# RWKV-7 scan: the decay's running sum over a chunk made by TensorE with a triangular matrix instead of by VectorE's scan, with a new order of the work around it

## What is computed

```python
w_lo = jnp.tanh(jnp.einsum("bld,zdr->zblr", xw, P["rw_w1"][j]))
w_raw = (P["rw_w0"][j][:, None, None, :] + jnp.einsum("zblr,zre->zble", w_lo, P["rw_w2"][j])).astype(f32)
decay = jnp.exp(-jnp.exp(-jax.nn.softplus(-w_raw) - 0.5))
...
def step(S, inp):
    r_t, w_t, k_t, v_t, a_t, b_t = inp
    sa = jnp.einsum("bhvk,bhk->bhv", S, a_t)
    S = S * w_t[:, :, None, :] + sa[..., :, None] * b_t[..., None, :] + v_t[..., :, None] * k_t[..., None, :]
    return S, jnp.einsum("bhvk,bhk->bhv", S, r_t)
```

## Time and profile before

| | |
|---|---|
| time, three runs | 3157.86, 3162.32, 3163.5 us; median 3162.32 us |
| profiled execution | 3172.32 us, span 3170.4 us |
| PE / PEld / DVE / ACT / POOL busy | 2754.4 / 1697.8 / 1449.8 / 729.9 / 246.5 us |
| stage of the scan | about 2030 to 2994 us of the span |
| mean granted TensorE clock | 0.932 of full |

### The profile page before, as it was taken

One profiled execution on the slowest core, in us unless ns is written; L12 is line 12 of the kernel. 1 busy time (PEld: TensorE's weight loads), 2 busy tenths in 40 slices (PEclk: granted clock), 3 DMA queues, 4 the chain that ended last, 5 costly groups with the idle time before them and its releaser, 6 DMA issues. The chain is left out here.

```text
span 3170.4 us, 73804 instructions
## 1 busy us (share of the span) xinstructions
PE 2754.4 (87%) x33234; PEld 1697.8 (54%) x33234; DVE 1449.8 (46%) x2139; ACT 729.9 (23%) x1264; POOL 246.5 (8%) x393
## 2 busy tenths in 40 slices
PE   7589999998999968939999999678888888898697
PEld 1155555554344434415555555367777777777543
DVE  0222222223999880051000000289898998988101
ACT  0122122221211110020000001244444545443100
POOL 0000000000000000000000000001121111111100
PEclk9789999998999989969999999789899999999698
DMA  6322222224223105113232323101111111110131
GB/s 239 132 78 83 88 88 84 88 86 133 67 67 100 58 13 194 45 47 102 79 104 86 99 94 97 52 28 32 34 42 38 34 45 35 41 34 27 66 142 60
DMA packets 208118, 242.59 MB, mean 77 GB/s; under 512 B 22439, under 2 KB 158135, under 8 KB 205544
## 3 DMA queue, kind: packets, MB, share of 16 engines
q1 hardware_dynamic: 197100, 196.56, 19.9%
q0 software_dynamic: 10752, 41.95, 3.6%
HBM read 184.97 MB, written 53.49 MB: 75 GB/s over the span
## 5 line engine op out<-in xcount | busy, mean ns | idle before, releaser
L104 PE MATMUL ps<-mix,rw 128*128 128x512 f32 (+1 forms) x2048 | 564.1, 439 | 21.7 <-DMA rw<-in_rw_w_v 5.7
L104 PE MATMUL ps<-hT,hw 128*128 128x512 f32 (+1 forms) x2048 | 561.3, 435 | 6.3 <-DMA hw<-in_hy_w_in 6.3
L104 PEld LDWEIGHTS ps<-mix,rw 128*128 128x128 f32 x2048 | 313.9, 194 | 271.9 <-issue 271.9
L104 PEld LDWEIGHTS ps<-hT,hw 128*128 128x128 f32 x2048 | 312.5, 191 | 252.4 <-issue 252.4
L104 PE MATMUL ps<-ow,oy 128*128 128x512 f32 x640 | 282.5, 604 | 27.5 <-DMA oy<-scratch_y_d 19.6
L1376 POOL TENSOR_SCALAR e_Sd<-e_S,e_pcd 128x64 f32<-128x64 f32 x256 | 163.7, 656 | 787.0 <-DVE e_S L107 319.2
L104 PEld LDWEIGHTS ps<-ow,oy 128*128 128x128 f32 x640 | 123.7, 194 | 185.2 <-issue 162.5
L118 ACT ACT_TABLE_LOAD x90 | 115.5, 1283 | 381.9 <-PE ps L104 276.1
L107 DVE SCALAR_TENSOR_TENSOR mix<-xx,col,hT 128x640 f32<-128x640 f32 x48 | 38.6, 879 | 287.5 <-PE ps L104 287.5
L112 DVE TENSOR_SCALAR hcv<-hpad,hpc 128x641 f32<-128x641 f32 x48 | 29.6, 616 | 305.7 <-ACT hpad L118 305.7
L115 DVE TENSOR_TENSOR rout<-ps,rsig 128x640 f32<-128x640 f32 x16 | 13.2, 824 | 275.2 <-ACT rsig L118 275.2
(11 more groups left out here) (205 smaller groups left out, 4168.8 us busy)
## 6 DMA issues: line engine op xcount, KB each, us to landing
hw<-in_hy_w_in SPq DMA_DIRECT2D x64, 512.0 KB, 4.1
aw<-in_ada_w SPq DMA_DIRECT2D x16, 1536.0 KB, 8.0
scratch_rkvz_d<-rout POOLq DMA_DIRECT2D x64, 320.0 KB, 3.4
scratch_vx_d<-hot POOLq DMA_DIRECT2D x32, 320.0 KB, 3.1
ow<-in_hy_w_out SPq DMA_DIRECT2D x32, 256.0 KB, 2.7
rw<-in_rw_w_r SPq DMA_DIRECT2D x16, 512.0 KB, 3.9
rw<-in_rw_w_k SPq DMA_DIRECT2D x16, 512.0 KB, 4.0
rw<-in_rw_w_v SPq DMA_DIRECT2D x16, 512.0 KB, 4.0
```

What stands on the lines that cost most here:

```text
L104: return nc.tensor.matmul(out, lhsT, rhs, start=first, stop=last)
```

## The change

The decay's raw rate is now made with tokens in the partitions: `rate(j, part)` takes a block of 128 tokens of `wlo` as weights and streams the 128 channels of `e_w2`, and adds the bias with a second product (a matrix with one row of ones per half, `first_rows`, and the row `e_w0`, which is loaded by two small transfers per unit). Both directions use their own half of the rows. `rate*` is one sigmoid of ACT over both directions (two, with the fifth block). `cum(j, d)` then multiplies each block of `e_sg` (as weights, tokens in the partitions) with a triangular matrix of ones within chunks, which gives the running sum with channels in the partitions again, in `wide`. `exps` takes it from there: it writes `e3` by reading the sum of the neighbouring token and puts 1 at the chunk's edge. `scan` is gone from DVE. `e_kr` for d = 0 moves from DVE to ACT (`kr0`). The load of `v` for the next unit waits for one more piece, and the first `e_w0` load waits for a memset of POOL.

```diff
-    ORDER = [("center*", 1), ("sums", 1), ("sb", 1, 0), ("sums*", 1), ("lora", 1, 0, 0), ("W*", 1, 0), ("sb*", 1, 1), ("U", 1, 0), ("std", 1),
...
+    ORDER = [("Z*", 1, 5), ("Q", 1), ("center*", 0), ("sums", 0), ("sb", 0, 1), ("W*", 0, 0), ("sb", 0, 0), ("sums*", 0), ("U", 0, 0), ("Sd", 0, 0),
...
+                    for d in range(2):
+                        sp.dma_start(w0[64 * d:64 * d + 1, :], A["rw_w0"][0, d:d + 1, ch(j)]).then_inc(s_l["w0"], 16)
...
+                def rate(j, part):
+
+                    wide_free("rate", j, part)
+                    pe.wait_ge(s_l["w2"], 16 * (j + 1))
+                    pe.wait_ge(s_l["w0"], 32 * (j + 1))
+                    for b in range(4) if part == 0 else (4,):
+                        for second in range(2):
+                            for d, hh in enumerate(HEADS):
+                                out = ps[:, WIDE + d, b % 4 * P:(b % 4 + 1) * P]
+                                if second:
+                                    last = mm(out, first_rows[hh, :], w0[hh, :], False, True)
+                                else:
+                                    mm(out, G["wlo"][hh, b * P:(b + 1) * P], lw2[hh, :], True, False)
+                    pe_.did(last, ("rate", j, part))
+
+                def sums_over_chunk(j, d):
+                    wide_free("cum", j, d)
+                    for part in range(2):
+                        wait(ac_, "took", "rate", j, part)
+                    for b in range(NT):
+                        last = mm(wide[:, b * P:(b + 1) * P], sg[:, d, b * P:(b + 1) * P], upto[d])
+                    pe_.did(last, ("cum", j, d))
...
+                def rate(j, part):
+                    wait(pe_, "rate", j, part)
+                    if j:
+                        for d in range(2):
+                            wait(dv_, "b", j - 1, d)
+                    at, n = (0, LS) if part == 0 else (LS, LP)
+                    ac_.did(act(sg[:, :, at:at + n], ps[:, WIDE:WIDE + 2, 0:n], ACT.Sigmoid), ("took", "rate", j, part))
...
+                    ac_.did(act(by_chunk(e3)[:, :, own], by_chunk(wide[:, 0:T])[:, :, prior], ACT.Exp, scale=-DECAY_MAX))
+                    ac_.did(act(by_chunk(e3)[:, :, edge], one.to_broadcast([P, NC]), ACT.Copy))
+                    ac_.did(act(e2[d][:, :], wide[:, 0:T], ACT.Exp, scale=DECAY_MAX), ("e2", j, d))
+                    ac_.did(act(e1, wide[:, 0:T], ACT.Exp, scale=-DECAY_MAX), ("exp", j, d))
+                    ac_.note(("took", "cum", j, d))
...
-                def scan(j, d):
-                    e1, e3 = ab[j % 3][:, 1, d, :], ab[j % 3][:, 0, d, :]
-                    for h in range(2):
-                        wait(ac_, "took", "lora", j, 0, h)
-                    if j >= 3:
-                        wait(pe_, "O", j - 3)
-                    dv_.did(vec.tensor_tensor_scan(e1, chunk, sg[d][:, :], 0.0, MUL, ADD), ("cum", j, d))
-                    wait(dv_, "cum", j, d)
-                    if d == 0:
-                        dv_.did(tt(e3, e1, sg[d][:, :], SUB), ("c", j, d))
-                    else:
-                        tot = chunks(e1)[:, :, C - 1:C].to_broadcast([P, NC, C])
-                        dv_.did(tt(chunks(e3), tot, chunks(e1), SUB), ("left", j))
-                        wait(dv_, "left", j)
-                        dv_.did(tt(e1, e3, sg[d][:, :], ADD), ("c", j, d))
```

More of the change, by code:

```diff
@@ L1161, in rwkv_scan @@
     T_ = lambda n: tab[:, TAB[n][0]:TAB[n][1]]
-    ident, heads, center, heads2, eye2, chunk = (T_(n) for n in ("ident", "heads", "center", "heads2", "eye2", "chunk"))
+    ident, heads, center, heads2, eye2, one, first_rows = (T_(n) for n in ("ident", "heads", "center", "heads2", "eye2", "one", "first_rows"))
+    upto = [T_("upto_f"), T_("upto_b")]
     between = T_("between").rearrange("p (l n) -> p l n", l=LEVELS)
@@ L1229, in rwkv_scan @@
                 jobs.append(piece)
-            if piece[0] in ("center", "lora", "sums", "spread", "bonus"):
+            if piece[0] in ("center", "rate", "cum", "lora", "sums", "spread", "bonus"):
                 wide_before[piece] = wide_last
@@ L1262, in rwkv_scan @@
         TAKER = {"sb": dv_, "sk": dv_, "V": ac_, "tb": ac_, "tk": ac_, "CT": ac_, "T": dv_, "Y": dv_, "Z": dv_, "O": ac_,
-                 "center": ac_, "lora": ac_, "sums": dv_, "spread": dv_, "bonus": dv_}
+                 "center": ac_, "rate": ac_, "cum": ac_, "lora": ac_, "sums": dv_, "spread": dv_, "bonus": dv_}
         def waiter(eng):
@@ L1313, in after_values @@
                         wait(pe_, "V", i)
+                        wait(dv_, "took", "bonus", i)
                         load_row("v", i + 1)
@@ L1317, in after_lora @@
                     if (q, h) == (1, 1) and j + 1 < KE:
-                        wait(pe_, "lora", j, 0, 1)
+                        wait(pe_, "rate", j, 0)
+                        wait(pe_, "rate", j, 1)
                         wait(pe_, "lora", j, 1, 1)
@@ L1580, in _ @@
                       "CT": turn_c, "T": turn_f, "Y": across, "Z": joined, "W": right_side, "U": solved, "S": next_state, "O": outputs,
-                      "fin": end_states, "center": centered, "lora": lora, "sums": sums, "spread": spread, "bonus": bonus})
+                      "fin": end_states, "center": centered, "rate": rate, "cum": sums_over_chunk, "lora": lora, "sums": sums, "spread": spread, "bonus": bonus})
             @block.scalar
@@ L1659, in lora @@
                         if j:
-                            wait(dv_, ("b", "k")[q], j - 1, d)
-                        bias = col_of(A0 + d, j) if q else col_w0(d, j)
-                        ac_.did(act((sg, ic)[q][d][:, half], ps[:, WIDE + d, 0:T // 2], ACT.Sigmoid, bias=bias), ("took", "lora", j, q, h))
+                            wait(dv_, "k", j - 1, d)
+                        ac_.did(act(ic[d][:, half], ps[:, WIDE + d, 0:T // 2], ACT.Sigmoid, bias=col_of(A0 + d, j)), ("took", "lora", j, q, h))
+                def rate(j, part):
[5 more added lines that the diff above has]
+                    ac_.did(act(sg[:, :, at:at + n], ps[:, WIDE:WIDE + 2, 0:n], ACT.Sigmoid), ("took", "rate", j, part))
                 def std(s):
@@ L1693, in _ @@
                 walk({"V*": take_v, "tb*": take_tb, "tk*": take_tk, "CT*": take_ct, "W*": right_side, "U*": solved, "O*": outputs,
-                      "fin*": end_states, "center*": centered, "keys": keys, "lora*": lora, "std": std, "wider": wider, "exps": exps,
-                      "ka": key_gain})
+                      "fin*": end_states, "center*": centered, "keys": keys, "lora*": lora, "std": std, "wider": wider, "rate*": rate,
+                      "exps": exps, "ka": key_gain, "kr0": first_gain})
             @block.vector
@@ L1820, in key_rate @@
                         wait(ac_, "took", "lora", j, 1, h)
-                    wait(dv_, "c", j, d)
-                    dv_.did(tt(sg[d][:, :], kk[:, :], ic[d][:, :], MUL), ("b0", j, d))
+                    wait(pe_, "cum", j, d)
+                    dv_.did(tt(sg[:, d, :], kk[:, :], ic[d][:, :], MUL), ("b0", j, d))
                 def key_dir(j, d):
@@ L1861, in bonus_in @@
                 def bonus_in(j):
-                    wait(dv_, "kr", j, 1)
+                    wait(dv_, "kr", j)
                     v_.wait_ge(s_l["r"], 16 * (j + 1))
@@ L1933, in constants @@
     put("chosen", np.concatenate([((row >> l) == (c >> l)) & np.where((row >> l) % 2 == 1, row <= c, row >= c) for l in levels], 1).astype(f))
-    put("chunk", np.tile((np.arange(T) % C != 0).astype(f), (P, 1)))
+    at, to = r[:, None], r[None, :]
+    for d, before in (("f", at <= to), ("b", at >= to)):
+        put(f"upto_{d}", (same & before).astype(f))
+    put("first_rows", np.tile(at % HID == 0, (1, P)).astype(f))
+    put("one", np.ones((P, 1)))
     put("sign", np.where(r[:, None] < HID, 1.0, -1.0))
```

57 lines of the change are left out of this document (31 added, 26 removed), and 27 rows, old and new, of the table ORDER.

## The result

| | before | changed |
|---|---|---|
| median (lowest to highest, runs) | 3161.68 us (3157.86 to 3163.5, 6) | 3185.9 us (3173.58 to 3189.55, 6) |
| profiled execution, its span | 3172.32, 3170.4 us | 3182.77, 3180.9 us |
| mean granted clock of the profiled execution | 0.932 | 0.939 |
| 14 full slots, from the first `e_Q` of one to that of the last | 2118.06 to 2893.99: 55.42 us each | 2119.82 to 2908.07: 56.30 us each |

The ratio is 1.0075, 95% interval 1.0056 to 1.0093: the change makes the kernel slower by 24 us. That was rival 3's sign and nearly its time (3189, slots of 56.5 us), not the forecast's 3156. The two profiled executions differ by 10.5 us of span only: before's was some 10 us over its median, the changed one 3 us under. What follows explains these 10.5 us. The other 14 us of the medians' 24 lie between executions of one kernel, and no profile here divides them.

What follows compares the result with a forecast made beforehand. TensorE was taken to bound the slot's head, DVE its middle. A slot's +3.7 - 3.4 - 0.7 - 0.5 + 0.2 = -0.7 us gave -10.5, the prologue +4.5: 3156 us from 3162.3, range 3130 to 3190.

Steps and rivals of the forecast that it cites:

- rival 3: In the slot, half of TensorE's waits for DVE stay and the clock gain fails: slot 56.5, 3189 us; chance 0.27.
- DVE's relief: In the slot, all TensorE waits for DVE go, -3.4 us, with tails -0.7; +0.2 put back for DVE's queue.
- Stops without releaser: TensorE stopping in the middle of pieces with nothing to wait for; held unchanged at 2.5 us a slot.
- TensorE's +3.7 us: Added TensorE work a slot: `rate` 2.6 and `cum` 2.6, less 1.5 for two replaced `lora` pieces.
- Rival 4: Weight loads or row halves don't overlap in `cum` and `rate`: +27 to +59 us, 3183 to 3215; chance 0.05.
- The clock: Half clock right behind TensorE's 1.89 us wait for `e_M2T` goes: -0.5 us a slot as mean gain.
- The prologue: Unit 0's preparation, with nothing beside it and TensorE at half clock, ends later: +4.5 us, between 0 and +9.
- DVE's 6.1 us: DVE work taken from the slot's middle: backward sum 3.12, forward sum 2.26, first `e_kr` 0.69 us.
- ACT's part: ACT's sigmoids, exponentials and `kr0` take it from 25.4 to about 26 us a slot, free as an amount.

Runs made afterwards that it cites:

- e5: The kernel before with the scan's five operations left out of DVE, the exponentials reading the sigmoids directly; 3150.39 us, ratio 0.9973.
- e4: The changed kernel's work put in the old order, with `cum` placed by hand; 3279.21 us, ratio 1.0364 to the kernel before.
- e12: The changed kernel with `lora` of the in-context rate, `center` and `bonus` cut into products of 128 and 64 columns; 3197.72 us, ratio 1.0104 to the kernel before.
- e8: The changed kernel with the bias of `rate` added by products over 512 columns for four blocks at once; 3169.99 us, ratio 1.0035 to the kernel before.
- e1: The changed kernel with `cum` cut to one block of five for each direction; 3185.02 us, ratio 1.0073 to the kernel before.
- e2: The changed kernel with the bias products of `rate` left out; 3168.13 us, ratio 1.0019 to the kernel before.
- e3: As a run: the work of the kernel before, put in the changed kernel's order; 3231.52 us, ratio 1.0209 to the kernel before.

## Why the prediction was wrong, step by step

- **DVE's relief (wrong, the failed step).** "If every wait of TensorE for DVE in the earlier trace rows went, these 3.4 us a slot go, and with them the tails", with "0.2 us back". Of 3.9 us net forecast, 2.7 came by the split above; by the profile's own lines the waits for DVE fell by 2.4 us a slot, where 3.4 were forecast. Waits for `e_M2T`, `e_kn` and `e_S` did go (below 0.5 us a slot, forecast below 1.5), but `e_Yi` came in with 0.8 us a slot. The step read DVE's 38.07 us of 38.6 in the earlier trace rows as proof that its queue, as an amount, is what TensorE waits for. This stretch holds both parts of the slot, and in the first of them TensorE was as full as DVE (8.02 of 8.62 us). `e5` shows that the amount over the slot doesn't decide: with 5.1 us a slot less on DVE the wait for `e_M2T` stays at 25 us, since the scans stood ahead of two S* that wait for TensorE, and the crowd ahead of T* stands behind these. The earlier trace rows had both: the scans at 2468.08 and 2473.70, each with an S* behind it, and the 1.89 us wait some 15 us later. In the old order the relief is worth 1.2 us a slot, not 4.4; the rest of the 2.7 us by which the waits fell is put to the new order by difference, and no run shows it by itself.
- **Stops without releaser (wrong, missing term).** They were held at 2.5 us a slot; they rose by 0.9 in the split, from 2.2 to 3.5 by the profile's lines. The text of rival 3 had the mechanism ("no longer hidden behind DVE's backlog"), the sum had nothing for it. The fourteen traces agree with it: few stops where TensorE waits for others, `e4` above all, and more where it doesn't. Whether the 103 instructions a slot more have a part in it beside that isn't shown; `e12` and `e8` speak for it, `e1` and `e2` don't.
- **TensorE's +3.7 us (right).** +3.65 by the accounting; `rate` 2.01 for four blocks and 0.65 for the fifth, `cum` 1.31. Rival 4 falls: the ten passes of `cum`, each with weights of its own over all rows, lie 0.11 us apart, as in the spread of the earlier trace rows. By the rule cited from the Trainium skill, TensorE: Matmul & The Clock Gate, section Part 3: Packing small matmuls, it would have been an estimated 2.2 us a direction; 1.31 was measured, so the trace disagrees with the rule here. The time of rival 4 was also added up wrongly: its +27 to +59 us already hold the forecast's -6, so they belong on top of before's 3162 (3189 to 3221) and not of the forecast.
- **The clock (right in kind, small in size).** The stretch at half clock behind the 1.9 us wait is gone: 2490.7 to 2494.1, which was at 0.50 in the earlier trace rows, is at full clock in the changed kernel, where it lies at the same place of its slot (36 us from the first `e_Q`). Of the 14 slots before, 9 have such a stretch 34 to 37 us from their start; none has in the changed kernel. The one at the slot's head stays. Worth 1.0 us a slot, priced 0.5.

```profile
2457.00:2461.00 4.00, 4.00 (x75) 3.88 (x71) 2.58 (x4) 1.40 (x2) 0.00 (x0) 0.63 0.01 4
2490.70:2494.10 3.40, 3.09 (x128) 2.72 (x128) 3.33 (x6) 2.19 (x4) 1.84 (x2) 1.00 0.02 5
```

- **The prologue (right in size where it was priced, less in the end).** The last preparation of unit 0 ends at 2068.7 us in place of 2064.2, +4.5 as forecast, but 0.9 of that was already there ahead of the stage's first `rate` (2038.97 against 2038.06), and the first `e_Q` comes only 1.7 us later: part of the delay was absorbed by what follows. The last full slot, 3.3 us shorter, wasn't forecast and is unexplained.
- **DVE's 6.1 us (nearly right).** Six operations a slot are gone; busy time fell by 5.2, since an operation behind a wait counts 0.82 us where one in a row takes 0.74 from start to start. ACT's part was right: 26.4 to 26.9 us a slot, and TensorE waits for it 0.2 us in 14 slots.
- **The range and rivals.** The time lies in the stated range and 3 us from rival 3, whose condition (more than 0.6 us of waits stay) was met: `e_Yi`, `e_M2T`, `e_S` and `e_bon` keep 1.4 us a slot by the profile. That the number is so near is luck in part: rival 3 had the clock gain fail, and it came (1.0 us a slot), while the stops, which its sum left out, rose by as much. More than half of the 24 us isn't seen in the profiled executions at all. The mistake of the forecast was to take one wait's releaser and the busy share of a long stretch together as the cause, without asking what DVE would meet first with the time that it is given.

What stays open: whether the stops are the supply of instructions (only their timing speaks for it), how `e8`'s gain divides between clock and instructions, why `e1` has more stops, what DVE's relief is worth in the new order, and what the best order for the changed work would give; `e3` and `e4` show only that orders can't be exchanged.

## What to carry to other kernels

Price an engine's relief piece by piece: time saved ahead of one of its own waits is lost in that wait, and only what is saved between its last wait and the operation that others want counts. A kernel that leaves the work out (here `e5`: 71 us less of DVE's work, 10 us less time) prices the relief, in its own order, before anything is moved. When work goes to TensorE, ask in which stretch it is the bound: 1.1 us of passes taken from the head gave 18 us back, 1.8 us taken from the middle nothing. And expect stops without a releaser to grow where waits for other engines go (31.4 to 48.3 us here). Last, look for the cheaper form on the engine that has the work: the scan from the row's end took away nearly half of what the change took off DVE, for no product at all, and gained what the whole relief could in that order.

## What the hardware showed that was not expected

TensorE stops in the middle of pieces without a releaser, up to 1.9 us at a time, 40 times in 14 slots before and 72 times after, 2.2 and 3.5 us a slot. All of the longer ones, over 0.3 us, begin 0.5 to 2.6 us behind the start of a 16 KB transfer of instructions, of which there is one for every 254 to 257 instructions of TensorE. 88 more instructions a slot cost nothing measurable in the kernel before (1.0009). A scan of 128x640 read and written with a negative step takes 1.50 us against 1.48 for the plain one.
